# Reordering the prologue of a two-layer hybrid trunk step: where the inputs are loaded, and in which order TensorE works through them

## What is computed

```python
m = jax.nn.silu(cond) @ w_mod + b_mod            # twice: cond = c_ctx and cond = c
y = xf * lax.rsqrt(jnp.mean(xf * xf, axis=-1, keepdims=True) + EPS) * g   # RMS norm of x
h = y * (1 + scale) + shift                      # shift, scale: parts of m
z = h @ w_in                                     # 1024 x 1536, the first projection
```

## Time and profile before

| | |
|---|---|
| median of 3 runs | 2024.88 us (2021.2 to 2025.21) |
| the profiled execution | 2022.2 us |
| its span, first to last instruction | 2020.6 us |
| PE busy | 1775.4 us, 88% of the span |
| DVE, ACT, POOL busy | 1331.7, 811.0, 284.4 us |
| DMA | 288.95 MB, mean 143 GB/s |
| chain that ended last, by engine | PE 74%, DVE 12%, issue 6%, ACT 4%, DMA 2% |

### The profile page before, as it was taken

One profiled execution on the slowest core, in us unless ns is written; L12 is line 12 of the kernel. 1 busy time (PEld: TensorE's weight loads), 2 busy tenths in 40 slices (PEclk: granted clock), 3 DMA queues, 4 the chain that ended last, 5 costly groups with the idle time before them and its releaser, 6 DMA issues.

```text
span 2020.6 us, 32486 instructions
## 1 busy us (share of the span) xinstructions
PE 1775.4 (88%) x11246; PEld 1591.8 (79%) x11247; DVE 1331.7 (66%) x2391; ACT 811.0 (40%) x1300; POOL 284.4 (14%) x280
## 2 busy tenths in 40 slices
PE   4898799999999999997377895699899899998992
PEld 1596399999999999994243593599888888998992
DVE  0577765667888886468886428444777688786446
ACT  1435424222122222323356525234654577753331
POOL 1000100000000000019940000101120121211012
PEclk9999899999999999997589997899999899998996
DMA  7434322535764343521000012235884799976334
GB/s 234 134 126 126 104 71 85 159 114 177 236 194 139 109 143 102 129 75 42 3 0 1 1 49 94 65 116 177 253 272 150 250 312 327 314 253 206 115 101 167
DMA packets 312634, 288.95 MB, mean 143 GB/s; under 512 B 20874, under 2 KB 301674, under 8 KB 312468
## 3 DMA queue, kind: packets, MB, share of 16 engines
q1 hardware_dynamic: 298292, 249.28, 39.9%
q0 software_dynamic: 12272, 34.50, 5.3%
q10 hardware_dynamic: 1904, 3.13, 0.5%
HBM read 263.38 MB, written 23.47 MB: 142 GB/s over the span
## 4 chain that ended last, share of the span: by engine, by line
PE 74%; DVE 12%; issue 6%; ACT 4%; DMA 2%; ACTq 1%; DVEq 0%; POOL 0%; POOLq 0%; SPq 0%
PE ps L1264 19%; PE ps L1265 18%; PE ps L1266 18%; PE ps L1269 5%; PE ps L1270 3%; PE ps L1376 2%; DVE vp L2404 2%; PE ps L1307 1%; DVE lo L2038 1%; PE ps L1326 1%; PE ps L1586 1%; ACT hi L770 1%; DMA raw<-in_moe_w_dram 1%; DVE hot L2640 1%; PE ps L1701 1%
## 5 line engine op out<-in xcount | busy, mean ns | idle before, releaser
L770 ACT ACTIVATE hi<-raw 128x1024 fp32r<-128x1024 f32 (+3 forms) x442 | 394.7, 919 | 522.6 <-PE ps L1266 450.1
L2038 DVE TENSOR_TENSOR lo<-raw,hi 128x1024 fp32r<-128x1024 f32 (+3 forms) x442 | 458.1, 1057 | 211.4 <-ACT hi L770 198.8
L1264 PE MATMUL ps<-h_wide,hi 128*128 128x320 f32 (+1 forms) x1728 | 542.1, 314 | 10.0 <-DVE h_wide L2153 5.5
L1266 PE MATMUL ps<-h_wide,lo 128*128 128x320 f32 (+1 forms) x1728 | 537.7, 311 | 0.0
L1265 PE MATMUL ps<-h_wide,hi 128*128 128x320 f32 (+1 forms) x1728 | 537.7, 311 | 0.0
L1264 PEld LDWEIGHTS ps<-h_wide,hi 128*128 128x128 f32 x1728 | 327.9, 190 | 12.8 <-issue 10.6
L1265 PEld LDWEIGHTS ps<-h_wide,hi 128*128 128x128 f32 x1728 | 327.6, 190 | 0.4 <-issue 0.2
L1266 PEld LDWEIGHTS ps<-h_wide,lo 128*128 128x128 f32 x1728 | 327.6, 190 | 0.0
L1264 PE MATMUL ps<-g_both,hi 128*128 128x320 f32 x528 | 166.8, 316 | 2.6 <-DVE g_both L2345 2.6
L1266 PE MATMUL ps<-g_both,lo 128*128 128x320 f32 x528 | 163.7, 310 | 0.0
L1265 PE MATMUL ps<-g_both,hi 128*128 128x320 f32 x528 | 163.7, 310 | 0.0
(11 more groups left out here) (381 smaller groups left out, 2828.0 us busy)
## 6 DMA issues: line engine op xcount, KB each, us to landing
raw<-in_moe_w_dram SPq DMA_DIRECT2D x160, 512.0 KB, 5.8
raw<-in_w_mod_dram SPq DMA_DIRECT2D x96, 512.0 KB, 4.5
raw<-in_moe_w_dram SPq DMA_DIRECT2D x96, 384.0 KB, 3.7
raw<-in_ff_w_dram SPq DMA_DIRECT2D x40, 512.0 KB, 4.8
raw<-in_moe_w_dram SPq DMA_DIRECT2D x64, 256.0 KB, 3.3
y_rows<-zeros POOLq DMA_DIRECT2D x22, 512.0 KB, 4.4
raw<-in_ev_w_in_dram SPq DMA_DIRECT2D x12, 512.0 KB, 5.6
raw<-in_ff_w_dram SPq DMA_DIRECT2D x16, 384.0 KB, 4.3
```

What stands on the lines that cost most here:

```text
L770: act.activation(hi[c % 2][:, parts[h]], raw[slot][:, parts[h]], ACT.Copy).then_inc(hi_done, 1)
L1264: pe.matmul(out, w_hi, v_hi, start=first, stop=False, skip_group_check=True)
L1266: return pe.matmul(out, w_lo, v_hi, start=False, stop=last, skip_group_check=True)
L2038: dve.tensor_tensor(lo[c % 2][:, parts[h]], raw[ring_of(c) % 4][:, parts[h]], hi[c % 2][:, parts[h]].bitcast(F32), ALU.subtract).then_inc( ...
```

## The change

- SP issues the five x tiles first, before any chunk of w_mod. Two semaphores tell of them: x_in for the first two tiles, x_more_in for the other three.
- ACT issues mats, then c_ctx and c into a tile of their own (crow, 16 rows), then the other 19 DMAs of small rows.
- PE waits for mats and crow, turns crow with one small transpose into PSUM bank 1, and goes on at once to the x transposes (the first four groups need only x_in). Then it does modulation chunks 0 and 1, norm_pe, and only then waits for the rows and turns prow. Chunks 2 to 7 follow in one go, then the projection.
- ACT makes cs straight from PSUM. Its order afterwards: copies of x, squares 0 to 3, modulation rows 0 and 1, squares 4 to 7, root, rows 2 and 3, the exp, the small router copy, rows 4 to 7, mod_keep(0), high part of EIN, shift and scaled x, high part of EIN + 1.
- DVE: clears, copies of x, norm_rs, par and the whole softplus, mod_params, low part of EIN, shift and scaled x, low part of EIN + 1.
- The semaphores prow_zero and ones_set become one, cleared.

```diff
+            for t in range(TT):
+                src = a["x_prompt"][0] if t == 0 else a["x_sample"][0, (t - 1) * P:t * P, :]
+                sp.dma_start(xrows[:, t, :], src).then_inc(x_in if t < 2 else x_more_in, 16)
+
             for c in range(6):
                 load(EIN + c, columns(a["ev_w_in"][0], c * 256))
...
             act.dma_start(mats[:, :, :], a["const_mats"].rearrange("m p c -> p m c")).then_inc(mats_in, 16)
-            for t in range(TT):
-                src = a["x_prompt"][0] if t == 0 else a["x_sample"][0, (t - 1) * P:t * P, :]
-                act.dma_start(xrows[:, t, :], src).then_inc(x_in, 16)
-            act.wait_ge(prow_zero, 1)
+            act.dma_start(crow[0:KT, :], a["c_ctx"].rearrange("(c p) -> c p", p=P)).then_inc(mats_in, 16)
+            act.dma_start(crow[KT:2 * KT, :], a["c"][0].rearrange("(c p) -> c p", p=P)).then_inc(mats_in, 16)
+            act.wait_ge(cleared, 1)
...
-                (1, CS, 8, a["c"][0].rearrange("(c p) -> c p", p=P)),
-                (1, CX, 8, a["c_ctx"].rearrange("(c p) -> c p", p=P)),
...
-            act.wait_ge(par_kept, 1)
-            act.activation(cs[:, :, 0], par[:, 1, CX:CX + KT], ACT.Silu)
-            act.activation(cs[:, :, 1], par[:, 1, CS:CS + KT], ACT.Silu).then_inc(cs_silu, 1)
-            act.wait_ge(ab_lam, 1)
-            act.activation(sm[:, 1, :], sm[:, 0, :], ACT.Exp, scale=-1.0).then_inc(ex_lam, 1)
+            act.wait_ge(par_turned, 1)
+            act.activation(cs[:, :, 0], ps[:, 1, 0:KT], ACT.Silu)
+            act.activation(cs[:, :, 1], ps[:, 1, KT:2 * KT], ACT.Silu).then_inc(cs_silu, 1)
...
+            for k in range(4):
+                square(0, k, (x_kept, 10))
+            mod_row(0, 2)
+            for k in range(4, KT):
+                square(0, k, (x_kept, 10))
+            root(0)
+            mod_row(2, 2)
+            act.wait_ge(ab_lam, 1)
+            act.activation(sm[:, 1, :], sm[:, 0, :], ACT.Exp, scale=-1.0).then_inc(ex_lam, 1)
             act.wait_ge(small_in, 16 * 14)
             act.activation(wr_hi[:, :, :], wr_raw[:, :, :], ACT.Copy).then_inc(wr_h, 1)
-
-            squares(0, lambda k: (x_kept, 10))
-            root(0)
+            mod_row(4, 4)
+            mod_keep(0)
             split_hi(EIN)
-            split_hi(EIN + 1)
-            mod_row(6, 2)
-            mod_keep(0)
             shift_hi(0, 0, 0)
             for k in range(KT):
                 scaled_hi(0, 0, k)
+            split_hi(EIN + 1)
...
-            pe.wait_ge(mats_in, 16)
-            pe.wait_ge(rows_in, 16 * 21)
-            for s in range(3):
-                last = pe.transpose(ps[:, 5, s * P:(s + 1) * P], prow[:, s, :], ident)
-            last.then_inc(par_turned, 1)
-
-            pe.wait_ge(cs_silu, 1)
-            pe.wait_ge(mats_in, 16)
-            mods(0, 4)
-
-            pe.wait_ge(x_in, 16 * TT)
+            pe.wait_ge(mats_in, 16 * 3)
+            pe.transpose(ps[:, 1, 0:2 * KT], crow[:, :], ident[0:2 * KT, 0:2 * KT]).then_inc(par_turned, 1)
+
             for g in range(10):
                 t, q = g // 2, g % 2
+                if g == 0:
+                    pe.wait_ge(x_in, 16 * 2)
+                elif g == 4:
+                    pe.wait_ge(x_more_in, 16 * (TT - 2))
                 if g >= 3:
                     pe.wait_ge(x_kept, g - 2)
...
-            mods(4, 2)
+            pe.wait_ge(cs_silu, 1)
+            mods(0, 2)
             norm_pe(0)
-            mods(6, 2, True)
+            pe.wait_ge(rows_in, 16 * 19)
+            for s in range(3):
+                last = pe.transpose(ps[:, 5, s * P:(s + 1) * P], prow[:, s, :], ident)
+            last.then_inc(par_turned, 1)
+            mods(2, 6, True)
...
             norm_rs(0)
+            dve.wait_ge(par_turned, 2)
+            dve.tensor_copy(par[:, :, :], ps[:, 5, 0:3 * P].rearrange("p (s c) -> p s c", s=3)).then_inc(par_kept, 1)
...
+            mod_params(0, part=0)
             split_lo(EIN)
-            split_lo(EIN + 1)
-            mod_params(0, part=0)
             shift_lo(0, 0, 0)
             for k in range(KT):
                 scaled_lo(0, 0, 0, k)
+            split_lo(EIN + 1)
```

More of the change, by code:

```diff
@@ L180, in hybrid_trunk_step @@
         prow = place("prow", [P, 3, P], at=scratch + 4 * TT * D)
+        crow = place("crow", [2 * KT, P], at=scratch + 4 * TT * D + 12 * P)
         off = scratch
@@ L293, in hybrid_trunk_step @@
         x_in = sem("x_in")
+        x_more_in = sem("x_more_in")
         rows_in = sem("rows_in")
@@ L303, in hybrid_trunk_step @@
         evac = sem("evac")
-        prow_zero = sem("prow_zero")
-        ones_set = sem("ones_set")
+        cleared = sem("cleared")
         x_turned = sem("x_turned")
@@ L794, in mod_keep @@
                 last.then_inc(mod_kept, 1)
-            mod_row(0, 4)
             for g in range(1, 10, 2):
@@ L803, in _ @@
                                ps[:, X_BANKS[g % 3], :].rearrange("p (k c) -> p k c", k=4), ACT.Copy).then_inc(x_kept, 1)
-            mod_row(4, 2)
             def square(i, k, ready):
@@ L2039, in split_lo @@
                                       ALU.subtract).then_inc(lo_done, 1)
[L2041 to L2050, removed]
+            dve.memset(prow[:, :, :], 0.0).then_inc(cleared, 1)
+            dve.memset(ones[:, :], 1.0).then_inc(cleared, 1)
+            dve.memset(wg[:, :, :], 0.0).then_inc(cleared, 1)
             for g in range(0, 10, 2):
@@ L2057, in _ @@
                                 ps[:, X_BANKS[g % 3], :].rearrange("p (k c) -> p k c", k=4)).then_inc(x_kept, 1)
[L2058 to L2073, removed]
             def mod_params(g, part=None):
@@ L2090, in mod_params @@
                 last.then_inc(mod_set, 1)
-            dve.wait_ge(wr_h, 1)
-            dve.tensor_tensor(wr_lo[:, :, :], wr_raw[:, :, :], wr_hi[:, :, :].bitcast(F32), ALU.subtract).then_inc(wr_l, 1)
             steps = [0]
@@ L2176, in _ @@
             norm_rs(0)
+            dve.wait_ge(par_turned, 2)
+            dve.tensor_copy(par[:, :, :], ps[:, 5, 0:3 * P].rearrange("p (s c) -> p s c", s=3)).then_inc(par_kept, 1)
+            dve.wait_ge(par_kept, 1)
+            dve.tensor_scalar(par[:, 1, QN:QN + 1], par[:, 1, QN:QN + 1], -HD ** -0.5, None, ALU.mult)
+            lam = par[:, 1, LAM:LAM + 8]
+            link(dve.tensor_scalar(sm[:, 2, :], lam, -1.0, None, ALU.mult))
+            dve.tensor_tensor(sm[:, 0, :], lam, sm[:, 2, :], ALU.max).then_inc(ab_lam, 1)
+            dve.wait_ge(ex_lam, 1)
+            link(dve.tensor_scalar(sm[:, 3, :], sm[:, 1, :], 2.0, None, ALU.add))
+            link(dve.reciprocal(sm[:, 3, :], sm[:, 3, :]))
+            link(dve.tensor_tensor(sm[:, 3, :], sm[:, 1, :], sm[:, 3, :], ALU.mult))
+            link(dve.tensor_tensor(sm[:, 4, :], sm[:, 3, :], sm[:, 3, :], ALU.mult))
+            link(dve.tensor_scalar(sm[:, 5, :], sm[:, 4, :], 1.0 / 15, None, ALU.mult))
+            for odd in (13, 11, 9, 7, 5, 3):
+                link(dve.scalar_tensor_tensor(out=sm[:, 5, :], in0=sm[:, 5, :], scalar=1.0 / odd, in1=sm[:, 4, :],
+                                              op0=ALU.add, op1=ALU.mult))
+            link(dve.scalar_tensor_tensor(out=sm[:, 5, :], in0=sm[:, 5, :], scalar=1.0, in1=sm[:, 3, :],
+                                          op0=ALU.add, op1=ALU.mult))
+            link(dve.tensor_scalar(sm[:, 5, :], sm[:, 5, :], 2.0, None, ALU.mult))
+            link(dve.scalar_tensor_tensor(out=sm[:, 5, :], in0=sm[:, 2, :], scalar=0.0, in1=sm[:, 5, :],
+                                          op0=ALU.max, op1=ALU.add))
+            dve.tensor_scalar(sm[:, 6, :], sm[:, 5, :], 8.0, None, ALU.mult)
+            dve.tensor_scalar(sm[:, 7, :], sm[:, 5, :], -8.0, None, ALU.mult).then_inc(sp_ready, 1)
+            dve.wait_ge(wr_h, 1)
+            dve.tensor_tensor(wr_lo[:, :, :], wr_raw[:, :, :], wr_hi[:, :, :].bitcast(F32), ALU.subtract).then_inc(wr_l, 1)
+            mod_params(0, part=0)
             split_lo(EIN)
-            split_lo(EIN + 1)
-            mod_params(0, part=0)
             shift_lo(0, 0, 0)
@@ L2870, in _ @@
                     link(dve.reciprocal(z_rs[:, t - 1:t], z_rs[:, t - 1:t]))
-                    dve.wait_ge(x_in, 16 * (TT + 1))
+                    dve.wait_ge(x_in, 16 * 3)
                     dve.scalar_tensor_tensor(out=rows_c[:, t - 1, 1, :], in0=rows_c[:, t - 1, 0, :], scalar=z_rs[:, t - 1:t], in1=norm_row[:, :],
@@ L2882, in _ @@
             pool.dma_start(wr_raw[:, :, :], a["moe_w_router"][0].rearrange("(k p) e -> p k e", p=P)).then_inc(small_in, 16)
-            pool.wait_ge(ones_set, 2)
+            pool.wait_ge(cleared, 3)
             for i, w in enumerate((a["a_w_r"], a["a_w_i"])):
```

## The result

The changed kernel takes 2045.24 us (median of 4 runs, 2042.73 to 2046.85) against 2025.05 us before: ratio 1.011 (1.009 to 1.013), slower by 20 us. The prediction said faster by 18 us.

A forecast was written before the change was run, and what follows sets the result against it. PE's 28 us wait for small rows behind full DMA engines was taken to bound the prologue. Moving the first projection matmul from 84.75 to 66.6 us saves 18.15 us: 2006 us forecast, range 2000.5 to 2012.5.

The forecast's parts named there:

- (a): Prologue loads: with x first in SP's queue, the last x tile lands at 16.0 us, chunk 0 at 19.2.
- (b): Prologue, ACT's queue: row issues end at 12.4 us, or 16.0 if a 3.7 us stall stays; 13 taken.
- (c): PE from x on: six x groups left at 16.0 us, PE slow at first; modulation chunks start at 21.5 us.
- (d): Rest of PE's prologue: chunks, sums and prow run without waits; last modulation chunk ends at 60.8 us, before at 78.7.
- (e): DVE and ACT beside PE: softplus ends at 54.0 us under PE's chunks, 7 us before mod_params, at no cost.
- (f): Prologue's tail: mod_keep at 61.6 us, first projection matmul at 66.6; 5.0 us against 5.2, with EIN's split now inside.
- (g): Behind the first projection matmul: the later split of EIN + 1 costs nothing; the rest moves as a whole.
- Rival 1: Prologue: crow lands late and holds PE's first instruction and the x transposes; 2008 to 2013 us; 0.17 beyond the forecast range.
- Rival 2: Prologue: x lands earlier, at 11 to 12 us, and chunk 0 could start at 18; 2002.5 us; 0.10 beyond the range.
- Rival 3: Prologue: chunk 0 or 1, or the chunks behind, land late and PE waits; 2012 to 2017 us; chance 0.07.
- Rival 4: Projection, slower than before: SP's ring refill with EIN + 3 comes late; 2029 us if landing takes 46 us; chance 0.02.
- Rival 5: Prologue: small rows or cs still hold PE, which starts at 28 us at worst; 2023 us; chance 0.02.

The follow-up runs named there:

- 64 and 92 copies: The changed kernel plus 64 or 92 one-element ACT copies, whose results nobody reads, ahead of ACT's expert loop: 2006.3 us with 64, 2048.6 us with 92.

## Why the prediction was wrong, point by point

- (a) When x is there: right. 16.0 us said, PE went on with x at 16.76.
- (b) ACT free at 13: it was 11.6, where its table load begins. The issue stall of 3.7 us at the first norm row was gone. The path did not notice, since x came later than ACT.
- (c) Start of the chunks at 21.5: measured 21.20. The slow first matmuls did not fall on the chunks: two took 7.07 us against the old 9.81. The granted clock of 10 to 20 us is 0.85, between the two levels of 1.2 and 2.4 GHz on average, and the x transposes took 3.67 and 4.51 us, 8.2 in all, against 6.55. So the slow part lay on them.
- (d) Right: mod_keep at 60.72 against 61.6. No wait for rows or refills.
- (e) Right: the softplus began at 46.9 and ended at 50.0, 11 us ahead of mod_params, not 7. The 6.3 us of the earlier trace rows held gaps that went.
- (f) Right: first matmul at 65.47 against 66.6, a tail of 4.8 us from mod_keep against 5.0. The split of EIN did take the place of the two splits.
- (g) First half right: EIN + 1 costs nothing, and the traces run in parallel, 19 us apart, for 1400 us. Its last sentence is the step that failed: "Past this point I see the same program with the same waits, moved as a whole." The sum of 18.15 us was right to 1.1 us, and a term of +42 us was missing from it, which is spent where ACT jumps: 5.0 to 5.2 us at the branch back to the loop's top ahead of each of four experts, and the rest at the other jumps beside it. The same instructions stand in the program, but not at the same addresses. I had costed ACT's five DMA issues as time in the prologue and not as five places in a program with a large loop behind it.
- *The rivals.* Rival 1: crow came at 9.6 us, within the bounds and without harm, while x was complete only at 16.8. So the rule that the prediction took from the Trainium skill (DMA: Bandwidth & Descriptors, "Queues, rings and completion order") would, as worked out there, have put crow too late; whether the rule or that working is off, no run here shows. Rival 2: x did not come early either. Rival 3: PE waited for no w_mod load in the first 110 us. Rival 4 was the one with the right sign, at 0.02, and its mechanism had no part: PE has no wait for a load of the projection there, and the traces run on 19 us apart. Rival 5: cs held PE nowhere.
- *What was to be seen beforehand.* The page of before has 81 packets of instructions, and ACT's timeline has idle time "until issue" of 8.3 us at the start of the fourth expert. These rows would have called for a rival; they do not give its price. Behind them stands a rule that the prediction did not use: the Trainium skill (Runtime: NRT & Kernel Launch, "Instruction fetch mechanics") says that a taken branch to code that is not loaded forces a fetch by DMA before execution goes on. By that rule a loop with large bodies that are jumped over is where a change of ACT's program length can cost, and the traces agree: 4.3 and 5.0 us around single jumps in the changed kernel, and 17.1 us for all those of one expert. They also show what the rule leaves open: at a good place the same jumps of the same expert leave ACT idle for only 1.7 us.

With that rival the forecast would have been two levels, near 2005 and near 2045 us. If the slow places are one stretch, at least 37 of 128 are slow, so the slow level would have deserved a chance of some 0.3 to 0.5 without a look at the addresses.

## What to carry to other kernels

An edit that adds or removes instructions on an engine moves all of its later code. Where that engine has a loop whose code comes to several packets of the instruction queue and that jumps, price this as a rival of its own, read the packets of the instruction queue and the idle time "until issue" before and after, and repeat a surprising result with a few harmless instructions ahead of the loop: here five of them were worth 40 us, twice the whole change. When a measured loss lies where nothing was edited, align the two traces on the same instruction and look for steps.

## What the runs showed of the hardware

- A packet of the instruction queue q14 is 8 KB (0.66 MB in 81). Time depends on where ACT's loop lies: a shift by one instruction took 48 us off (2053.2 to 2005.5 us, single runs), and a shift by 128 was slow like none (2043.6 and 2045.2 us).
- With the loop at a good place, no instruction packet came on q14 from 1640 to 1750 us, through the fifth and sixth expert; at a bad one 9 came, and at the beginning of the third, fifth, sixth and seventh expert 9 to 12 us each were lost.
- The jumps missed one by one: 4.3, 5.0, 2.7 and 3.2 us in one expert, the first two with the DMA engines full (372 and 350 GB/s from 1465 to 1475 us), the other two with little traffic (91 GB/s from 1476 to 1482 us). The branch back to the loop's top alone took 5.0 to 5.2 us at four experts of the changed kernel and 0.2 us at the same four of the kernel before.
- The hint that names the target of the jump back is worth 49 us in this kernel at a good place (2054.4 us without, 2005.7 with it).
- Not settled: whether the number of pieces that the loop touches or the place of one part of it decides, and where between 64 and 92 copies the slow stretch begins. What the same shift does to DVE's and PE's loops was not tried; their programs did not change in length or by one instruction.
